# A transformer kernel: roots of the norms on four partition groups

## The reference, cut to what matters

```python
# first block, twice per layer: RMS norm, then modulation by a condition
y = x32 * lax.rsqrt(jnp.mean(x32 * x32, axis=-1, keepdims=True) + EPS)
return h * (1 + scale) + shift
# second block: layer norm, once at the entry and twice per layer
mu = jnp.mean(xf, axis=-1, keepdims=True)
var = jnp.mean(jnp.square(xf - mu), axis=-1, keepdims=True)
y = (xf - mu) * lax.rsqrt(var + LN_EPS)
return (y * g.astype(jnp.float32) + b.astype(jnp.float32)).astype(x.dtype)
```

## Time and profile before

| | us |
|---|---|
| median of three executions | 3436.25 |
| lowest, highest | 3435.07, 3437.97 |
| profiled execution, its own time | 3432.84 |
| its span, first to last instruction | 3431.1 |
| mean granted TensorE clock | 0.983 |

### The profile page before, as it was taken

The page is one execution under the profiler, slowest core; times in us unless marked ns, Lnnn a source line. Parts: engine busy times, 40 slices in busy tenths (PEclk is TensorE's granted clock), DMA queues, the critical chain, the costliest instruction groups (busy, mean ns, idle before and its releaser), DMA issues.

```text
span 3431.1 us, 39924 instructions
## 1 busy us (share of the span) xinstructions
PE 3263.2 (95%) x16116; PEld 2571.7 (75%) x16116; DVE 1446.1 (42%) x2552; ACT 1307.0 (38%) x2299; POOL 1408.2 (41%) x798
## 2 busy tenths in 40 slices
PE   7988999999998889999999999999999989989997
PEld 4864788888864446788886688878887668868886
DVE  5556342222236654321233766243222658444132
ACT  4222242212244665432333534343333543444243
POOL 2224433222242434444463136634455225554446
PEclk9999999999999999999999999999999999999999
DMA  6134212121133000323232020322323111122322
GB/s 228 62 142 178 109 53 68 53 72 56 54 111 118 13 13 13 138 85 109 83 114 99 19 83 24 103 104 86 111 80 123 50 46 56 47 86 87 104 87 67
DMA packets 85635, 286.04 MB, mean 83 GB/s; under 512 B 9771, under 2 KB 10347, under 8 KB 84940
## 3 DMA queue, kind: packets, MB, share of 16 engines
q1 hardware_dynamic: 85452, 283.50, 24.2%
HBM read 281.37 MB, written 2.10 MB: 83 GB/s over the span
## 4 chain that ended last, share of the span: by engine, by line
PE 86%; DVE 7%; ACT 4%; DMA 2%; issue 1%; POOL 1%; SPq 0%; DVEq 0%; ACTq 0%
PE ps L457 20%; PE ps L460 20%; PE ps L458 20%; DMA ring<-in_w_mod 2%; PE ps L497 2%; PE ps L1919 2%; PE ps L498 2%; PE ps L499 2%; PE ps L526 1%; PE ps L1989 1%; PE ps L1173 1%; PE ps L1963 1%; PE ps L2313 1%; PE ps L2327 1%; PE ps L2805 1%
## 5 line engine op out<-in xcount | busy, mean ns | idle before, releaser
L409 POOL TENSOR_TENSOR WL<-ring,WH 128x1024 fp32r<-128x1024 f32 (+2 forms) x443 | 959.8, 2170 | 1504.3 <-ACT WH L400 1503.8
L457 PE MATMUL ps<-HX,WH 128*128 128x512 f32 x1768 | 695.3, 393 | 5.6 <-POOL WL L409 5.6
L460 PE MATMUL ps<-HX,WL 128*128 128x512 f32 x1768 | 692.2, 391 | 0.0
L458 PE MATMUL ps<-HX,WH 128*128 128x512 f32 x1768 | 690.7, 391 | 0.0
L400 ACT CAST WH<-ring 128x1024 fp32r<-128x1024 f32 (+2 forms) x443 | 420.4, 951 | 365.6 <-PE ps L460 317.0
L457 PE MATMUL ps<-FR,WH 128*128 128x512 f32 x1120 | 418.7, 374 | 0.3
L458 PE MATMUL ps<-FR,WH 128*128 128x512 f32 x1120 | 409.5, 373 | 0.0
L457 PEld LDWEIGHTS ps<-HX,WH 128*128 128x128 f32 x1768 | 332.8, 188 | 84.1 <-POOL WL L409 7.7
L460 PE MATMUL ps<-FR,WL 128*128 128x512 f32 x1120 | 389.2, 373 | 0.0
L460 PEld LDWEIGHTS ps<-HX,WL 128*128 128x128 f32 x1768 | 334.0, 189 | 49.6
L458 PEld LDWEIGHTS ps<-HX,WH 128*128 128x128 f32 x1768 | 333.1, 188 | 49.3
(11 more groups left out here) (378 smaller groups left out, 5122.2 us busy)
## 6 DMA issues: line engine op xcount, KB each, us to landing
ring<-in_w_mod SPq DMA_DIRECT2D x96, 512.0 KB, 5.4
ring<-in_ffn_w_up SPq DMA_DIRECT2D x88, 512.0 KB, 3.3
ring<-in_w_up SPq DMA_DIRECT2D x88, 512.0 KB, 3.2
ring<-in_w_in_tok SPq DMA_DIRECT2D x40, 512.0 KB, 3.3
ring<-in_w_in_feat SPq DMA_DIRECT2D x32, 512.0 KB, 3.2
ring<-in_ffn_w_down SPq DMA_DIRECT2D x32, 384.0 KB, 3.1
ring<-in_w_out SPq DMA_DIRECT2D x32, 384.0 KB, 3.1
ring<-in_w_down SPq DMA_DIRECT2D x32, 384.0 KB, 3.1
```

Of the source, the lines that this page charges most:

```text
L409: pool.tensor_tensor(WL[:, p % SPLITS, 0:n], ring.ap(r), WH[:, p % SPLITS, 0:n], ALU.subtract).then_inc(*ring.frees(r, split.g, "low", p))
L457: pe.matmul(o, high, xh, first, False)
L458: pe.matmul(o, high, xl, False, False)
L460: m = pe.matmul(PS[bs[i]][:, 0:N], low, get(k)[0], False, last)
```

## The change

All nine norms take their roots of token quarters. A product with 32 columns of ones (`quarters_pe`) writes the sums of token quarter g to partitions 32g to 32g+31, so that 512 tokens stand on 128 partitions x 128 columns (64 more columns for the context, in the same bank). Root, reciprocal and, in the layer norms, the variance are taken on that. `whole_pe` spreads the result again: for each quarter a product whose stationary operand is one column of the identity, repeated 128 times, writes it to all partitions of a PSUM bank; DVE then reads the root from PSUM rather than from SBUF. In the layer norms the sum of x is made twice, once on whole rows for the mean and once in quarters for its square (on ACT); the sums' order on PE is new; `off_v` subtracts the mean from tiles 0 and 1 on DVE, from PSUM, and POOL does the other six.

```diff
-        def some_pe(pe, c0, n):
+        def some_pe(pe, c0, n, sts):
             b = bank.take("mod_n", c0)
             pe.wait_ge(*bank.free("mod_n", c0))
             for c in range(c0, c0 + n):
                 rows_pe(pe, c)
-                if c > c0:
+                if c == c0:
+                    whole_pe(pe, sts)
+                else:
...
+        def first_sums_pe(pe, sts):
+            b = bank.take("sum", sts[0].name)
+            pe.wait_ge(*bank.free("sum", sts[0].name))
+            for s, q in enumerate(sts):
+                pe.wait_ge(*nm.v.at("first", q.name, 7))
+                m = quarters_pe(pe, b, 128 * s, T[:, s, 0:q.N], q.N, True, True)
+            m.then_inc(*nm.pe.up("total", sts[0].name))
 
         def totals_pe(pe, sums):
+
+            b = bank.take("sum", sums[0])
+            pe.wait_ge(*bank.free("sum", sums[0]))
             for s, name in enumerate(sums):
-                N = (S, SC)[s]
-                total_pe(pe, name, 6 + s, N, T[:, 4 + (7 * len(sums) + s) % 2, 0:N], nm.a.at("square", name, 7))
+                pe.wait_ge(*nm.g.at("add", name, 6))
+                quarters_pe(pe, b, 128 * s, T[:, 6 + s, 0:(S, SC)[s]], (S, SC)[s], True, False)
+                pe.wait_ge(*nm.a.at("square", name, 7))
+                m = quarters_pe(pe, b, 128 * s, T[:, 4 + (7 * len(sums) + s) % 2, 0:(S, SC)[s]], (S, SC)[s], False, True)
+            m.then_inc(*nm.pe.up("total", sums[0]))
...
+        def quarters_pe(pe, b, at, src, N, first, last):
+            w = N // 4
+            for g in range(4):
+                m = pe.matmul(PS[b][32 * g:32 * g + 32, at:at + w], ones[:, 0:32], src[:, g * w:g * w + w], first, last)
+            return m
+
+        def whole_pe(pe, sts):
+            pe.wait_ge(*nm.v.at("inverse", sts[0].name))
+            for s, q in enumerate(sts):
+                w = q.N // 4
+                b = bank.take("whole", q.name)
+                pe.wait_ge(*bank.free("whole", q.name))
+                for g in range(4):
+                    m = pe.matmul(PS[b][:, g * w:g * w + w], ident[:, 32 * g:32 * g + 1].to_broadcast([128, 128]),
+                                  T[:, 0, 128 * s:128 * s + w], True, True)
+                m.then_inc(*nm.pe.up("whole", q.name))
+
+        def root_v(dve, sts):
+            name, w = sts[0].name, sum(q.N for q in sts) // 4
             dve.wait_ge(*nm.pe.at("total", name))
-            dve.tensor_scalar(T[:, r, 0:N], ps("sum", name)[:, 0:N], 1.0 / DD, eps, ALU.mult,
+            dve.tensor_scalar(T[:, 0, 0:w], ps("sum", name)[:, 0:w], 1.0 / D, EPS, ALU.mult,
                               ALU.add).then_inc(*bank.emptied(("sum", name), nm.v, "ms", name))
-        def root_a(act, name, N, r):
+        def root_a(act, sts):
+            name, w = sts[0].name, sum(q.N for q in sts) // 4
             act.wait_ge(*nm.v.at("ms", name))
-            act.activation(T[:, r, 0:N], T[:, r, 0:N], ACT.Sqrt).then_inc(*nm.a.up("root", name))
-
-        def inverse_v(dve, name, N, r):
+            act.activation(T[:, 0, 0:w], T[:, 0, 0:w], ACT.Sqrt).then_inc(*nm.a.up("root", name))
+
+        def inverse_v(dve, sts):
+            name, w = sts[0].name, sum(q.N for q in sts) // 4
             dve.wait_ge(*nm.a.at("root", name))
-            dve.reciprocal(T[:, r, 0:N], T[:, r, 0:N]).then_inc(*nm.v.up("inverse", name))
+            dve.reciprocal(T[:, 0, 0:w], T[:, 0, 0:w]).then_inc(*nm.v.up("inverse", name))
...
-                dve.wait_ge(*nm.v.at("inverse", q.name))
+                dve.wait_ge(*nm.pe.at("whole", q.name))
             dve.wait_ge(*nm.v.now())
             for j, (k, s) in enumerate(items):
                 if inplace:
-                    dve.wait_ge(*nm.g.at("off", sts[0].name, k))
+                    dve.wait_ge(*(nm.v if k < OFF else nm.g).at("off", sts[0].name, k))
                 if j >= 4 and not inplace:
                     dve.wait_ge(*(nm.g if in_pool(sts, *items[j - 4], inplace) else nm.v).at("low", name, j - 4))
                 q = sts[s]
-                dve.scalar_tensor_tensor(part_d(sts, j, k, s, inplace), q.src(k), q.gain(k), T[:, q.r, 0:q.N], ALU.mult,
-                                         ALU.mult).then_inc(*nm.v.up("scaled", name, j))
+                root = ps("whole", q.name)[:, 0:q.N]
+                up = nm.v.up("scaled", name, j) if k < 7 else bank.emptied(("whole", q.name), nm.v, "scaled", name, j)
+                dve.scalar_tensor_tensor(part_d(sts, j, k, s, inplace), q.src(k), q.gain(k), root, ALU.mult,
+                                         ALU.mult).then_inc(*up)
                 if j >= nst:
...
+        OFF = 2
+
         def ln_pe(pe, q, done):
-            total_pe(pe, q.name, 6, S, X[:, 7, :], done, "mean")
-            total_pe(pe, q.name + "2", 7, S, T[:, 5, :], nm.a.at("square", q.name, 7))
+            name = q.name
+            mean, first, second = (bank.take(x, name) for x in ("mean", "first", "sum"))
+            for x in ("mean", "first", "sum"):
+                pe.wait_ge(*bank.free(x, name))
+            pe.wait_ge(*nm.g.at("add", name, 6))
+            pe.matmul(PS[mean][:, :], ones[:, :], T[:, 6, :], True, False)
+            quarters_pe(pe, first, 0, T[:, 6, :], S, True, False)
+            pe.wait_ge(*nm.g.at("add", name + "2", 6))
+            quarters_pe(pe, second, 0, T[:, 7, :], S, True, False)
+            pe.wait_ge(*done)
+            quarters_pe(pe, first, 0, X[:, 7, :], S, False, True).then_inc(*nm.pe.up("first total", name))
+            pe.matmul(PS[mean][:, :], ones[:, :], X[:, 7, :], False, True).then_inc(*nm.pe.up("mean", name))
+            pe.wait_ge(*nm.a.at("square", name, 7))
+            quarters_pe(pe, second, 0, T[:, 5, :], S, False, True).then_inc(*nm.pe.up("total", name))
+
+        def off_v(dve, q, k):
+
+            dve.wait_ge(*nm.a.at("mean", q.name))
+            up = nm.v.up("off", q.name, k) if k < OFF - 1 else bank.emptied(("mean", q.name), nm.v, "off", q.name, k)
+            dve.scalar_tensor_tensor(X[:, k, :], ps("mean", q.name)[:, :], -1.0 / D, X[:, k, :], ALU.mult,
+                                     ALU.add).then_inc(*up)
 
         def spread_v(dve, q):
-            mean = ps("mean", q.name)[:, :]
-            dve.wait_ge(*nm.a.at("mean", q.name))
-            dve.scalar_tensor_tensor(T[:, 2, :], mean, 1.0 / D, T[:, 1, :], ALU.mult, ALU.mult).then_inc(
-                *bank.emptied(("mean", q.name), nm.v))
+            t = T[:, 0, 0:128]
+            dve.wait_ge(*nm.a.at("square of mean", q.name))
+            dve.wait_ge(*nm.pe.at("total", q.name))
+            dve.scalar_tensor_tensor(t, ps("sum", q.name)[:, 0:128], 1.0 / D, T[:, 2, 0:128], ALU.mult,
+                                     ALU.subtract).then_inc(*bank.emptied(("sum", q.name), nm.v))
             dve.wait_ge(*nm.v.now())
-            dve.wait_ge(*nm.pe.at("total", q.name + "2"))
-            dve.scalar_tensor_tensor(T[:, 0, :], ps("sum", q.name + "2")[:, :], 1.0 / D, T[:, 2, :], ALU.mult,
-                                     ALU.subtract).then_inc(*bank.emptied(("sum", q.name + "2"), nm.v))
-            dve.wait_ge(*nm.v.now())
-            dve.tensor_scalar(T[:, 0, :], T[:, 0, :], 0.0, LN_EPS, ALU.max, ALU.add).then_inc(*nm.v.up("ms", q.name))
-            inverse_v(dve, q.name, S, 0)
+            dve.tensor_scalar(t, t, 0.0, LN_EPS, ALU.max, ALU.add).then_inc(*nm.v.up("ms", q.name))
+            off_v(dve, q, 0)
+            inverse_v(dve, [q])
+            off_v(dve, q, 1)
 
         def mean_a(act, q):
+            act.wait_ge(*nm.pe.at("first total", q.name))
+            act.activation(T[:, 2, 0:128], ps("first", q.name)[:, 0:128], ACT.Square, scale=1.0 / D).then_inc(
+                *bank.emptied(("first", q.name), nm.a, "square of mean", q.name))
             act.wait_ge(*nm.pe.at("mean", q.name))
             act.mul(T[:, 1, :], ps("mean", q.name)[:, :], 1.0 / D).then_inc(*nm.a.up("mean", q.name))
 
         def ln_g(pool, q):
-            for k in range(8):
+            for k in range(OFF, 8):
                 pool.wait_ge(*nm.a.at("mean", q.name))
                 pool.tensor_tensor(X[:, k, :], X[:, k, :], T[:, 1, :], ALU.subtract).then_inc(*nm.g.up("off", q.name, k))
...
-        def mem_keys_pe(pe, l):
+        def mem_keys_pe(pe, l, between):
             for n in range(4):
+                if n == 1:
+                    between()
...
-            mem_keys_pe(pe, 0)
+            mem_keys_pe(pe, 0, lambda: whole_pe(pe, [ln_in]))
...
-                    mem_keys_pe(pe, 1)
+                    mem_keys_pe(pe, 1, lambda: whole_pe(pe, [ln_1[0]]))
+                else:
+                    whole_pe(pe, [ln_1[1]])
...
-                    mem_values_pe(pe, 1)
+                    mem_values_pe(pe, 1, lambda: whole_pe(pe, [ln_2[0]]))
+            whole_pe(pe, [ln_2[1]])
...
-            dve.wait_ge(*nm.v.now())
+            dve.wait_ge(*nm.pe.at("whole", ln_2[1].name))
             for k in range(8):
```

(20 more changed lines are left out.)

43 lines of the change are left out of this document (14 added, 29 removed).

## The result

The changed kernel takes 3447.75 us (median of six runs, 3444.28 to 3450.8) against 3434.65 us (six runs, 3433.0 to 3437.97) for the kernel before: a ratio of 1.0041 with a 95% interval of 1.0030 to 1.0051. The forecast was 3428.1. It is slower by 13 us where it was to be faster by 8. The profiled execution has a span of 3446.3 us, 15.2 more than before.

The account below looks back on a forecast made before the run. PE, busy 95% of the span, was taken as the bound. -2.7 (n2) - 3.3 (ln_1[1]) - 3.9 (the end) + 1.8 (covered norms) = -8.1 us: 3428.1 us on the median, range 3421.5 to 3436.

Parts of the forecast that it names:

- Other first-block work: First-block norms: earlier sums and roots gain nothing, two spreads fit between rows; 0, or up to 1 us cost each.
- covered norms: ln_in, ln_1[0] and ln_2[0], where memory products keep PE busy: shorter sums against added spreads, +1.8 us (0 to +4).
- Root in PSUM: DVE's scaling reads one SBUF operand instead of two, so DVE and POOL stop blocking each other there; all of it taken.
- in line: Rival, chance 0.07: the four quarter places do not run at once, 0.64 us more a set; sum +4.0, 3440.3 us.
- A set of quarters: Eight PE instructions, 32 columns of weights by 128, at four places: 0.22 us, against 0.86 for one whole sum.
- ln_1[1]: Behind this norm, scaling and low part come earlier although the mean is 0.7 us later: -3.3 us (-2 to -5).
- A spread: Eight PE instructions of 128 x 128 weights: 0.95 us a stream, about 1.7 at half clock, plus 0.3 until DVE sees it.
- n2: Behind n2 DVE's turn falls from 2.21 to 1.73 us and PE's waits shrink: -2.7 us (0 to -3.3).
- n3: Behind n3, one stream and no such waits as behind n2: 0.
- The end: Behind ln_2[1], eight scalings take 5.4 us instead of 7.91 and end earlier: -3.9 us (-3 to -5).
- quick chain: Rival, chance 0.18: small L836 wins against POOL and PE spreads at full clock; -12.2 us in all, 3424.
- The page on tiling modes: Mode change drains PE; waiting for whole tails costs 0.7 us more per layer norm, gain 3 us smaller; forecast used 0.1.

Follow-up runs that it names:

- the banks put right: Changed kernel with only the order of PSUM banks at n0 and n1 and the place of one ACT copy changed: 3423.31 us, ratio 0.9976 to before.
- the waits alone: Kernel before with only three PE waits added, behind n0, n1 and ln_in, and nothing of the change: 3473.37 us, ratio 1.0125.
- the spread later: Kernel with the banks put right, but the spread of n1, n2 and n3 one quarter of a w_mod row later: 3425.83 us, ratio 0.9982.

## Why the prediction was wrong, by its steps

- **The step that failed** is "Other first-block work ... 0" and the price of the covered norms, +1.8. Both summed PE's products, the engines' turns and the copies, and never asked which PSUM bank each product gets and who empties it. "Root in PSUM" was costed for what it frees and not for what it holds: a bank, from the spread to the last scaling. No rival spoke of it, and the rival that was slower, "in line", had another mechanism. It was there to be read, in `take` and `free`, and "where a stall goes, what is late next" should have been put for banks too. What the runs showed in its place: PE waits 6.0, 8.0 and 5.5 us for a bank and then steps at half clock, +8.3 at `n0`, most of 11.0 at `n1` and 8.1 of 10.3 at `ln_in`; with the banks put right the loss is gone, and the waits alone bring one.
- **A set of quarters** was right and the rival "in line" fell: two sets of 128 columns take 0.46 us at `ln_1[1]` (L663 at 3054.59 and 3055.05 above), 0.23 each where 0.22 stood. (By the rival's own terms, 12.1 us for 0.64 in a set, the change would have turned to a loss at 0.65 us, not at 0.62.) At `n1` one set of 128 columns and two of 64, 0.47 us to the first row:

```profile
422.69 0.65 PE L663 MATMUL ps<-T,ones 128*32 128x128 f32 x24 [1.15 <-ACT T L869]
423.16 1.90 PE L526 MATMUL ps<-ring,cs 128*32 128x512 f32 x16
...
427.00 2.00 PE L673 MATMUL ps<-T,ident 128*128 128x128 f32 x16 [1.94 <-DVE T L691]
```

- **A spread** is 1.0 us a stream (0.95), 16 instructions in 2.0 for two. That this fits between the rows was wrong: PE stands 1.94 us at L673. The cover was read too long: the 20 instructions of the earlier trace rows hold four of the second row, and the first row alone, the 16 above, lasts 1.90 us and not 2.77; nor was its end moved by the 1.2 us that it starts earlier. And the spread starts 3.84 us behind the rows, where the inverse was put at 3.5: ACT casts weights for 1.03 us (L400 at 422.85) ahead of the table load. The price, up to 1 us a norm, was sized about right all the same: from the end of `L_out`'s pair to the pair behind `n1` it is 66.2 to 67.4 us with the new `n1` and 65.7 to 66.2 with the old. With the banks right a further 1.2 us lies in the pair (19.7 against 18.4), where PE stays at half clock for longer; in the kernel with the spread later it does not (18.6), and why is open.
- **Reciprocal**: 0.86 us from start to start for 128 columns, 0.87 forecast.
- **`n2`**: DVE's turn went from 2.21 to 1.72 us (1.73) and the stretch lost 3.0 (-2.7). Right.
- **`n3`** was put at 0 and gave 2.5: 1.2 between the pairs and 1.2 in its own, which has fewer steps at half clock. The forecast counted only waits there and none of the slow steps; what raised the clock is not settled. The pair's part does not come every time: it takes 11.4 us in the changed kernel and with the banks right, and 12.65 with the spread later, as before (12.64).
- **`ln_1[1]`** -3.9 for -3.3, with DVE's L836 held by POOL (1.24 us for 128 columns), the upper end of what was put for it. **The end** -4.6 for -3.9: PE's spread took 1.0, not 2, though it had stood for 3.2 us. That PE would spread at half clock held in some kernels and not in this one; to that extent it went the way of the "quick chain", which wanted L836 free of POOL as well and did not get it.
- **The covered norms**: from the first sum to the product behind the keys or values it is 0.95 us more at `ln_in`, 0.5 at `ln_1[0]` and 1.05 at `ln_2[0]`, +2.5 in all for +1.8. The sums are 0.5 shorter where 0.7 was put, the spreads cost 1.0 at `ln_1[0]` and 1.5 at the other two, with a wait of 0.2 us at L673 in it where 0.5 stood. But `ln_1[0]` gained 3.6 behind its pair, outside the window of 25 us. Before, PE stood there for POOL's low part of the weights:

```profile
PE ps L457 <- POOL WL L409: 2.8, 1, 2.8
```

That hung on ACT, which came to the first unit's result 2 us behind the end of the pair (2244.25), late from the norm's parts:

```profile
2246.22 0.79 ACT L853 ACTIVATE T<-ps,pv 128x512 f32<-128x512 f32 x1
```

The other 1.2 us are steps at half clock that stood behind this wait (granted clock 0.50 from 2252.6 to 2256.0 before). All eight kernels with the new layer norms gain 3.6 to 3.9 us here. Now ACT is through with the norm first and waits for PE there, and the wait for POOL is 0.4 us:

```profile
2271.96 0.78 ACT L898 ACTIVATE T<-ps,pv 128x512 f32<-128x512 f32 x1 [2.28 <-PE ps L437]
```

- **The page on tiling modes**: the Trainium skill (TensorEngine Tiling (Array Packing), Key Properties) says that a change of the tiling mode drains the engine. At `ln_1[1]` the turn from the sum to the quarters takes 0.10 us beyond two steps of 0.43 (L812 at 3053.63, L663 at 3054.59), the one back 0.10 (L663 at 3055.05, a set of 0.23, L818 at 3055.38), the next 0.19 (L663 at 3056.43). 0.4 for a norm's turns was the right size; the 0.17 more for a wait for a whole tail shows in full at none of the three. The row decided rightly.

That the banks put right come out at -8.7 us where -8.1 was forecast is partly luck: in its profile 3.6 at `ln_1[0]` and 2.5 at `n3` were missed on one side, some 2 each at `n0` and `n1` and 4 by chance of the clock on the other (the profiled run took 3427.3 us, and its span is 5.6 us below that of before).

## What to carry to other kernels

An operand that moves to PSUM takes a bank for as long as its last reader needs, and every bank given out behind it is another one: after a change in the number of banks, list for each product on the critical engine which buffer it gets and who empties that, and when. A wait whose releaser has nothing to do with the instruction's inputs is a wait for a buffer; rotating the buffers, or moving one small copy forward, took it away here. And read what stands behind a covered stretch, not only the stretch.
